# Six more output pieces kept as halves, and a wait ahead of GpSimd's second piece set

## The chip, the cores and the metric

The kernel runs on one core of a Trainium2 chip. The metric is the device time of one execution in microseconds, the median of three runs. Lower is better.

## What is computed

One layer of a mixer over 4096 frames of 1024 channels, then a last norm. Cut to what matters here:

```python
h = rms_norm(x, norm_w) * (1.0 + scale) + shift
gq, gk, gv, gz, glr, hq, hf, hi, hz, mg = split(h @ w_in)
# two gated linear recurrences over chunks of 64 frames; their decays:
log_a = log_sigmoid(glr @ gla_wa2 + gla_ba) / 16
log_f = logaddexp(log(lb), log1p(-lb) + log_sigmoid(hf))
g_a, g_b = split(sigmoid(mg + merge_b))
m = g_a * (o_g @ w_up_gla) + g_b * (o_h @ w_up_hgrn)
x = x + gate * (m @ w_out)          # 1024 x 1024, the "output" product
return rms_norm(x, final_norm_w)
```

## The kernel before

The 4096 frames are 8 blocks of 512. In each block TensorE walks through 75 slots. A slot is one weight tile of 128 partitions x 1024 numbers (512 KB) and the matmuls that use it. Slots 0 to 3 are hf, 4 and 5 gk, 6 to 9 hi, 10 to 13 gv, 14 and 15 gq, 16 to 19 hq, 20 to 27 the gates, 28 to 60 the merge gates and the up projections, and 61 to 74 (`OUT0` is 61) the output product. Slots 0 to 33, 59 and 60 hold 24 matmuls each (5.44 us); an output slot holds 12 (2.72 us). The 14 output slots are seven products of a Strassen-like scheme, two slots (q = 0, 1) for each: the first three multiply parts of m, the other four sums of them.

All matmuls are fp32r with each operand as a high and a low half, three products for each pair. So each weight tile needs two halves in SBUF, `w_hi` and `w_lo`, each a ring of 3 (`RING`). They come in one of two ways:

- From raw: SyncE (SP) loads the tile into `w_raw` (ring of 4, `RAW`), ScalarE copies it to `w_hi` (`split_hi`, L748) and VectorE subtracts to get `w_lo` (`split_lo`, L1024). Both do this right after the slot three places before has ended (`slot_done`). SP loads the tile that stands four raw uses ahead, when the split of the tile of this slot is done (`w_split`).
- From halves: in block 0 the split halves of the slots in `HALVES` are stored to DRAM (`keep_halves`, two stores of 512 KB at the slot, ahead of the raw load of that slot, L429). In later blocks `load_halves` (L444) brings them back, two loads of 512 KB, issued when the slot three places before has ended. Then ScalarE and VectorE do nothing for the tile. ScalarE's split of slot s in block 0 waits until the halves of slot s - 3 have been stored (`halves_kept`), since it overwrites them.

SP's queue is in order: what stands behind a wait is issued after it. In each block it also loads, around the output slots, the next block's transposed x (`xf`, two pairs at slots 55 and 58 and one at 63) and the residual `xy`, 512 KB for each of four frame tiles: two at slot 63 after `up_used`, two at slot 65 after `s_lo_done`. In `body` of SP the steps of one slot stand in this order: raw load, load of halves, xf, xy.

VectorE adds the finished output banks into `xy` (`bank_adds`, L1158). The first two adds stand at slot 64, behind the split for slot 67, and wait for the first two xy loads. TensorE's slot 67 waits for these two adds (`BANK_READ[3]` is 2), slot 69 for four, slot 71 for eight.

The weights of the output slots are not the input's: GpSimd makes them in block 0 (`out_pieces`), multiplied with the gate and combined, and stores 14 pieces to DRAM (`pieces`). It makes two sets, q = 0 and q = 1, each with four loads, eight elementwise operations on 128 x 1024 numbers and seven stores. The buffer `w_b` lies where ScalarE writes `o_tm` from slot 21 on.

The decays are worked out in slots 4 to 16, by ScalarE and VectorE in turn. TensorE's running sums of them are hosted behind slots 14, 15 (L1679, L1680) and 16 (L1687, L1688); those of slot 15 wait for VectorE's `pk` (L1302), which reads the bank. Near the end of that chain VectorE writes `la_lo` (L1286, slot 13), which is `la_split`.

## Time and profile before

| | us |
|---|---|
| median of 3 runs | 2816.75 (2815.58 to 2817.88) |
| profiled execution, its own time | 2816.22 |
| its span, first to last instruction | 2814.5 |
| TensorE busy in the span | 2771.9 |
| VectorE busy | 1708.7 |
| ScalarE busy | 1332.2 |
| GpSimd busy | 402.6 |

The profiled execution lies 0.5 us under the median and 1.7 us over its span. TensorE is busy 98% of the span, the DMA queue of SP takes 52.3% of the 16 DMA engines' time. Lines as L1583 are lines of the kernel before.

### The profile page before, as it was taken

The page shows a single profiled execution, that of the slowest core. Times are in us where ns is not written, and L with a number is a line of the kernel's source. Part 1 is how long each engine was busy: PE and PEld are TensorE (multiplying, and loading weights), DVE is VectorE, ACT ScalarE, POOL GpSimd, SP SyncE. Part 2 cuts the span into 40 slices and gives each one's busy share as a digit, 9 for nine tenths or more (in the row PEclk, how much of TensorE's full clock was granted, in tenths as well). Part 3 has the DMA queues.
Part 4 walks back from the last instruction along what each step waited for, and adds up shares of the span by engine and source line. Part 5 has one row for each costly group of instructions (what it writes and reads, how often), then busy time and mean ns, then how long its engine had stood idle before and what let it go on. Part 6 is the DMA issues. An engine that isn't in the chain of part 4 may idle for free.

```text
span 2814.5 us, 39321 instructions
## 1 busy us (share of the span) xinstructions
PE 2771.9 (98%) x15840; PEld 2339.1 (83%) x15840; DVE 1708.7 (61%) x2269; ACT 1332.2 (47%) x1854; POOL 402.6 (14%) x451
## 2 busy tenths in 40 slices
PE   6999999999999999999999999999999999999998
PEld 4778888889887898879888798888988889888897
DVE  7855484476744766547655577545675366744666
ACT  4643356344472454724547244463454534544344
POOL 1625310111001110011000110001101011000111
PEclk9999999999999999999999999999999999999999
DMA  9768574445734447344573456734566344653444
GB/s 375 284 237 300 203 246 181 151 156 166 256 135 165 152 169 271 124 163 155 191 277 108 148 160 213 244 125 142 163 214 234 128 149 152 227 187 136 149 154 176
DMA packets 154134, 532.34 MB, mean 189 GB/s; under 512 B 16288, under 2 KB 16544, under 8 KB 152416
## 3 DMA queue, kind: packets, MB, share of 16 engines
q1 hardware_dynamic: 147072, 505.50, 52.3%
q0 software_dynamic: 6624, 24.12, 2.4%
q8 instruction: 126, 2.06, 0.3%
q14 instruction: 56, 0.46, 0.0%
q10 hardware_dynamic: 256, 0.20, 0.0%
HBM read 473.85 MB, written 55.71 MB: 188 GB/s over the span
## 4 chain that ended last, share of the span: by engine, by line
PE 87%; ACT 5%; DVE 5%; issue 2%; DMA 1%; SPq 0%; POOL 0%; POOLq 0%; DVEq 0%; ACTq 0%
PE A L1458 28%; PE F L1469 16%; PE A L1561 10%; PE A L1583 7%; PE F L1500 6%; PE R L1500 5%; PE A L1500 3%; PE F L1458 3%; PE F L1583 2%; PE R L1613 1%; DVE w_lo L1024 1%; ACT w_hi L748 1%; PE F L1640 1%; PE A L1655 1%; PE F L1634 1%
## 5 line engine op out<-in xcount | busy, mean ns | idle before, releaser
L1024 DVE TENSOR_TENSOR w_lo<-w_raw,w_hi 128x1024 fp32r<-128x1024 f32 x423 | 550.2, 1301 | 397.1 <-ACT w_hi L748 395.8
L748 ACT ACTIVATE w_hi<-w_raw 128x1024 fp32r<-128x1024 f32 x423 | 446.9, 1057 | 494.9 <-PE R L1500 149.7
L1458 PE MATMUL A<-w_hi,h_hi 128*128 128x512 f32 (+1 forms) x1408 | 532.8, 378 | 0.0
L1458 PE MATMUL A<-w_lo,h_hi 128*128 128x512 f32 (+1 forms) x1408 | 523.1, 371 | 0.0
L1458 PE MATMUL A<-w_hi,h_lo 128*128 128x512 f32 (+1 forms) x1408 | 522.8, 371 | 0.0
L1458 PEld LDWEIGHTS A<-w_hi,h_hi 128*128 128x128 f32 x1408 | 264.4, 188 | 55.8 <-issue 8.7
L1458 PEld LDWEIGHTS A<-w_hi,h_lo 128*128 128x128 f32 x1408 | 264.4, 188 | 46.6
L1458 PEld LDWEIGHTS A<-w_lo,h_hi 128*128 128x128 f32 x1408 | 264.7, 188 | 42.8 <-issue 0.2
L1469 PE MATMUL F<-h_hi,w_hi 128*128 128x512 f32 x736 | 290.7, 395 | 0.0
L1469 PE MATMUL F<-h_lo,w_hi 128*128 128x512 f32 x736 | 287.3, 390 | 0.0
L1469 PE MATMUL F<-h_hi,w_lo 128*128 128x512 f32 x736 | 287.3, 390 | 0.0
L1561 PE MATMUL A<-o_hi,w_hi 128*128 128x512 f32 x512 | 199.4, 390 | 0.0
L1561 PE MATMUL A<-o_lo,w_hi 128*128 128x512 f32 x512 | 199.4, 390 | 0.0
L1561 PE MATMUL A<-o_hi,w_lo 128*128 128x512 f32 x512 | 199.2, 389 | 0.0
L1469 PEld LDWEIGHTS F<-h_hi,w_hi 128*128 128x128 f32 x736 | 138.7, 188 | 29.5 <-DVE w_lo L1024 0.4
L1469 PEld LDWEIGHTS F<-h_hi,w_lo 128*128 128x128 f32 x736 | 138.4, 188 | 29.3
L1469 PEld LDWEIGHTS F<-h_lo,w_hi 128*128 128x128 f32 x736 | 138.6, 188 | 28.1 <-issue 0.2
L601 POOL TENSOR_TENSOR rstd<-ssq,eps_t 128x4 f32<-128x4 f32 x64 | 33.9, 530 | 760.4 <-DVE ssq L1347 760.4
L1216 DVE TENSOR_TENSOR gates<-gates,A 128x512 f32<-128x512 f32 x128 | 82.2, 683 | 78.4 <-PE A L1561 78.4
L691 POOL TENSOR_TENSOR m_raw<-m_raw 128x256 f32<-128x256 f32 x24 | 24.2, 1007 | 704.4 <-DVE m_lo L1233 704.4
L1334 DVE SCALAR_TENSOR_TENSOR S_h<-S_h,a_cols,R 128x128 f32<-128x128 f32 x256 | 71.9, 343 | 78.8 <-PE R L1613 77.6
L881 ACT ACTIVATE gates<-F,col 128x512 f32<-128x512 f32 x44 | 30.3, 688 | 185.1 <-PE F L1469 185.1
(278 smaller groups left out, 5651.2 us busy)
## 6 DMA issues: line engine op xcount, KB each, us to landing
w_raw<-in_w_stream SPq DMA_DIRECT2D x225, 512.0 KB, 3.9
w_hi<-halves SPq DMA_DIRECT2D x154, 512.0 KB, 3.7
w_lo<-halves SPq DMA_DIRECT2D x154, 512.0 KB, 4.6
w_raw<-pieces SPq DMA_DIRECT2D x112, 512.0 KB, 5.3
w_raw<-m_pieces SPq DMA_DIRECT2D x84, 512.0 KB, 3.5
xy<-in_x SPq DMA_DIRECT2D x32, 512.0 KB, 6.5
result<-xy SPq DMA_DIRECT2D x32, 512.0 KB, 8.1
xf<-in_xt SPq DMA_DIRECT2D x30, 512.0 KB, 5.3
```

What stands on the lines that cost most here:

```text
L601: nc.gpsimd.tensor_tensor(dst, src, eps_t[:, 0:k], ALU.add).then_inc(pool_pow, 1)
L748: AF(w_hi[:, s % RING, 0:n], w_raw[:, r, 0:n], ACT.Copy).then_inc(w_hi_done, 1)
L881: AF(gates[:, j % 2, g, :], F[g][:, :], ACT.Sigmoid, bias=merge_b[:, g * KT + FEAT[j]:g * KT + FEAT[j] + 1]).then_inc(mg_used.sem, 1)
L1024: V.tensor_tensor(w_lo[:, s % RING, 0:n], w_raw[:, u % RAW, 0:n], w_hi[:, s % RING, 0:n].bitcast(fp32), ALU.subtract).then_inc(w_split, 1)
L1216: ins = V.tensor_tensor(gates[:, j % 2, g, :], gates[:, j % 2, g, :], A[2 * (j % 2) + g][:, :], ALU.mult)
L1334: ins = V.scalar_tensor_tensor(out=S_h[:, c, g, :], in0=S_h[:, 1 - c, g, :], scalar=a_cols[:, g, n:n + 1], in1=R[c][:, g * P:(g + 1) * P], ...
L1458: last = mm(banks[t][:, 0:width], src[ia][:, k, t * P:(t + 1) * P], w_[iw][:, s % RING, kk * width:(kk + 1) * width], start=(k == 0 and n ...
L1469: last = mm(dst[:, :], w_[iw][:, s % RING, k * P:(k + 1) * P], h_[ia][:, k, :], start=(k == 0 and n == 0), stop=(k == KT - 1 and n == 2))
L1500: last = mm(dst, w_[iw][:, s % RING, 512 * g + kk * P:512 * g + (kk + 1) * P], src[ia][:, kk // 2, kk % 2, :], start=(n < 4 and kk == 0 an ...
L1561: last = mm(A[2 * (j % 2) + g][:, :], w_[iw][:, s % RING, kk * P:(kk + 1) * P], o_[ia][:, kk, :], start=(k == 0 and n == 0), stop=(k == HE ...
L1583: last = mm(OUT_BANK[pair_][tt][:, :], src[ia][:, 2 * (2 * q + kk) + f, at:at + P], w_[iw][:, s % RING, kk * 512:(kk + 1) * 512], start=(f ...
L1613: last = mm(R[c][:, g * P:(g + 1) * P], kdec_h[fr, t, g * P:(g + 1) * P], v_h[fr, t, g * P:(g + 1) * P], start=True, stop=True)
```

## The change

`HALVES` grows by slots 61 to 66, `KEPT` and the DRAM tensor by the output slots; SP's one wait in block 1 now covers all stores. So in block 0 SP stores 12 more halves of 512 KB, at slots 61 to 66. In blocks 1 to 7 the six raw loads from `pieces`, the six copies on ScalarE and the six subtractions on VectorE go, and 12 loads of halves come. Separately, GpSimd waits for block 0's `la_split` before the first multiplication of its second set; the four loads of that set are issued before the wait.

```diff
-KEPT = range(RING, OUT0)
-HALVES = (*range(3, 10), *range(20, 36), 60)
+KEPT = range(RING, SLOTS)
+HALVES = (*range(3, 10), *range(20, 36), *range(60, 67))
...
-        halves = nc.dram_tensor("halves", [OUT0 - RING, 2, P, SLOT_W], fp32, kind="Internal").ap()
+        halves = nc.dram_tensor("halves", [SLOTS - RING, 2, P, SLOT_W], fp32, kind="Internal").ap()
...
-                                sp.wait_ge(halves_kept[r], 32 * stored_on(OUT0 + (r - OUT0) % RING))
+                                sp.wait_ge(halves_kept[r], 32 * stored_on(SLOTS + r))
...
+                    if q:
+                        pool.wait_ge(la_split.sem, la_split.at(0, 1))
                     for i, piece in ((0, B11), (2, B21), (3, B22)):
                         gated(i, q)
                         store(i, piece + q)
```

SP's queue in block 0 around the first output slots, before (the `xf` at the top stands at slot 60; `halves<-` is a store, `w_raw<-` a load):

```order
L455 DMA xf<-in_xt 128x1024
L423 DMA w_raw<-pieces 128x1024 x3
L455 DMA xf<-in_xt 128x1024
L555 DMA xy_106<-in_x 128x1024 x2
L423 DMA w_raw<-pieces 128x1024 x2
L555 DMA xy_107<-in_x 128x1024 x2
```

The same place now, up to the stores of slot 64:

```order
L455 DMA xf<-in_xt 128x1024
L429 DMA halves<-w_hi 128x1024
L429 DMA halves<-w_lo 128x1024
L423 DMA w_raw<-pieces 128x1024
L429 DMA halves<-w_hi 128x1024
L429 DMA halves<-w_lo 128x1024
L423 DMA w_raw<-pieces 128x1024
L429 DMA halves<-w_hi 128x1024
L429 DMA halves<-w_lo 128x1024
L423 DMA w_raw<-pieces 128x1024
L455 DMA xf<-in_xt 128x1024
L555 DMA xy_106<-in_x 128x1024 x2
```

Two stores of 512 KB now stand ahead of each raw load of slots 61 to 66.

SP's queue in a later block around the same slots, before (`w_hi<-halves` and `w_lo<-halves` are the load for slot 60; the second `xf` stands at slot 63):

```order
L444 DMA w_hi<-halves 128x1024
L444 DMA w_lo<-halves 128x1024
L423 DMA w_raw<-pieces 128x1024
L455 DMA xf<-in_xt 128x1024
L423 DMA w_raw<-pieces 128x1024 x4
L455 DMA xf<-in_xt 128x1024
L555 DMA xy_106<-in_x 128x1024 x2
L423 DMA w_raw<-pieces 128x1024 x2
L555 DMA xy_107<-in_x 128x1024 x2
```

Now, from the load for slot 63 on:

```order
L444 DMA w_hi<-halves 128x1024
L444 DMA w_lo<-halves 128x1024
L444 DMA w_hi<-halves 128x1024
L444 DMA w_lo<-halves 128x1024
L444 DMA w_hi<-halves 128x1024
L444 DMA w_lo<-halves 128x1024
L444 DMA w_hi<-halves 128x1024
L444 DMA w_lo<-halves 128x1024
L455 DMA xf<-in_xt 128x1024
L555 DMA xy_106<-in_x 128x1024 x2
L555 DMA xy_107<-in_x 128x1024 x2
L423 DMA w_raw<-pieces 128x1024 x4
```

The four pairs are the halves of slots 63 to 66, each behind a wait for the end of slots 60 to 63, and `xf` and `xy` now stand behind the last of these waits.

## Rows read from the trace of the kernel before

**Rows 1.** The page, part 1: busy us, share of the span, instructions.

```profile
PE 2771.9 (98%) x15840; PEld 2339.1 (83%) x15840; DVE 1708.7 (61%) x2269; ACT 1332.2 (47%) x1854; POOL 402.6 (14%) x451
```

**Rows 2.** Waits of TensorE over the whole span: us in total, times, longest.

```profile
PE R L1679 <- DVE pk L1302: 5.0, 1, 5.0
PE F L1583 <- DVE w_lo L1024: 2.7, 7, 0.4
```

**Rows 3.** The chain, slot 65 of blocks 2 and 3: start, us, what.

```profile
1060.15 5.73 PE F L1583 x24
...
1403.74 5.73 PE F L1583 x24
```

**Rows 4.** Stretches: slots 14-17 of blocks 0, 1; output slots of blocks 2, 7.

```profile
core 0: us, PE busy (x) PEld busy (x) DVE busy (x) ACT busy (x) POOL busy (x), PEclk, DMA share, GB/s
129.40:150.43 21.03, 16.02 (x65) 12.83 (x64) 15.49 (x10) 9.62 (x13) 19.04 (x13) 0.84 0.61 221
484.80:498.87 14.07, 14.07 (x64) 11.41 (x65) 8.65 (x10) 9.91 (x14) 0.00 (x0) 1.00 0.21 76
1048.29:1087.84 39.55, 39.04 (x169) 31.38 (x169) 36.72 (x44) 22.17 (x26) 0.10 (x1) 1.00 0.74 252
2764.79:2803.00 38.21, 38.19 (x168) 31.11 (x167) 30.25 (x36) 19.43 (x23) 0.74 (x2) 1.00 0.50 170
```

**Rows 5.** Timeline of VectorE, block 0 (126 to 142), then block 1.

```profile
126.83 3.42 DVE L1296 SCALAR_TENSOR_TENSOR y_g<-y_g,t 128x1024 f32<-128x1024 f32 x1
...
140.15 1.40 DVE L1302 SCALAR_TENSOR_TENSOR pk<-R,keep,pk 128x512 f32<-128x512 f32 x2
...
484.67 1.22 DVE L1296 SCALAR_TENSOR_TENSOR y_g<-y_g,t 128x1024 f32<-128x1024 f32 x1
```

**Rows 6.** Timeline of GpSimd, first and last of the second set's eight operations.

```profile
125.45 3.72 POOL L638 TENSOR_TENSOR w_b<-w_b,gate_bc 128x1024 f32<-128x1024 f32 x1 [1.51 <-DMA w_b<-in_w_stream]
...
149.98 2.42 POOL L659 TENSOR_TENSOR w_b<-w_b 128x1024 f32<-128x1024 f32 x1
```

**Rows 7.** Timeline of SP, slots 57 to 65 of block 2: start, us, issue.

```profile
1034.55 0.32 SPq L444 DMA_DIRECT2D w_hi<-halves  x1
1034.91 0.43 SPq L444 DMA_DIRECT2D w_lo<-halves  x1
...
1053.85 0.91 SPq L555 DMA_DIRECT2D xy<-in_x  x2
```

**Rows 8.** The page, part 6: DMA issues, KB each, median us to landing.

```profile
w_lo<-halves SPq DMA_DIRECT2D x154, 512.0 KB, 4.6
```

**Rows 9.** DMA issues from 853.5 to 854.4: one pair of halves.

```profile
w_lo<-halves SPq DMA_DIRECT2D x1, 512.0 KB, 6.3
```

**Rows 10.** Timeline of VectorE, block 2: the first adds into xy.

```profile
1064.55 1.28 DVE L1158 TENSOR_TENSOR xy<-xy,A 128x512 f32<-128x512 f32 x2
```

**Rows 11.** Timeline of TensorE: first matmuls of slots 61, 67 (block 2), 69 (block 0).

```profile
1048.29 0.47 PE L1583 MATMUL A<-w_hi,m_hi 128*128 128x512 f32 x1
...
1065.98 0.47 PE L1583 MATMUL A<-w_hi,s_hi 128*128 128x512 f32 x1
...
384.32 0.39 PE L1583 MATMUL A<-w_hi,s_hi 128*128 128x512 f32 x1
```

**Rows 12.** DMA issues from 355 to 356, block 0: the xf of slot 60.

```profile
xf<-in_xt SPq DMA_DIRECT2D x1, 512.0 KB, 6.4
```

**Rows 13.** Stretches of block 0 with a full DMA queue, columns as rows 4.

```profile
60.00:98.00 38.00, 38.00 (x213) 32.36 (x212) 26.34 (x27) 19.73 (x25) 11.08 (x9) 1.00 1.00 370
74.00:94.00 20.00, 20.00 (x104) 16.95 (x104) 9.84 (x8) 11.87 (x17) 7.17 (x7) 1.00 1.02 397
57.00:73.00 16.00, 16.00 (x94) 14.06 (x93) 13.84 (x19) 6.54 (x9) 0.21 (x1) 1.00 0.95 333
```

**Rows 14.** The page, part 5: groups, busy us, mean ns, idle before and what ended it.

```profile
L1024 DVE TENSOR_TENSOR w_lo<-w_raw,w_hi 128x1024 fp32r<-128x1024 f32 x423 | 550.2, 1301 | 397.1 <-ACT w_hi L748 395.8
L748 ACT ACTIVATE w_hi<-w_raw 128x1024 fp32r<-128x1024 f32 x423 | 446.9, 1057 | 494.9 <-PE R L1500 149.7
```

## The prediction

> **What bounds the kernel now.** I read the page's busy times first. TensorE is busy 2771.9 us of a span of 2814.5 [rows 1], so an edit can give back little: only the time in which it stands or runs at half clock. The chain shows slot 65 of blocks 2 and 3 at 1060.15 and 1403.74 [rows 3]: a steady block takes 343.59 us, and its end costs no more than what lies between its slots. Then I read the waits of TensorE [rows 2]. Past the start of the program, whose waits the change doesn't touch, two belong to it: one of 5.0 us in block 0, on VectorE's `pk`, and seven of 0.4 us on a weight split, at slot 65 of a block each. Last I read stretches. The part of slots 14 to 17 takes 21.03 us in block 0 and 14.07 in block 1 with the same matmuls; its clock is 0.84 against 1.00, so after it had stood TensorE ran for a while at 1.2 GHz in place of 2.4 [rows 4]. The 14 output slots take 39.55 us in block 2 and 38.21 in block 7, where no next block is prepared; 14 slots of 2.72 would be 38.1. So the first edit can give back at most some 1.45 us a block, the second at most 21.03 - 14.07 = 6.96 us, once.
>
> **The wait on GpSimd.** In block 0 VectorE's operations with two inputs in SBUF take 3.42 us beside GpSimd's second set, the same operation in block 1 takes 1.22; `pk`, with one input in a bank, keeps its 0.70 each [rows 5]. GpSimd's set starts at 125.45 and ends at 152.4 [rows 6]. Now it starts at `la_split`. Without it, `y_g` ends at 126.83 + 1.22 = 128.05, the next split at 129.3, and `la_lo` (after ScalarE's copy of about 1.1) near 130.6. That is where the set now starts. The split for slot 17 still falls beside it: it starts near 131.2, takes 3.4, and two `pk` of 1.40 end near 136.0. TensorE comes to them at 135.8 and waits 0.2 to 0.8 us in place of 5.0, and its clock stays up. Gain: **6.2 us**. If slot 16's `pk` is late in the same way and part of the half-clock stretch stays, it is 4; at best 7. The set ends 5.2 us later, with its last store near 161. ScalarE needs the buffer in slot 21, after 170, and SP needs the pieces at slot 57: neither waits.
>
> **The six splits that go, in blocks 1 to 6.** They free ScalarE and VectorE of six operations each a block, and with them the 0.4 us of slot 65. Their end has its price in SP's queue. The halves of slot s are loaded when slot s - 3 has ended. For slots 63 to 66 only two output slots of 2.72 us lie between, 5.44 us. SP issues 0.2 us after the end of a slot; `w_lo` is issued 0.36 after `w_hi` [rows 7] and lands 4.6 after that [rows 8]: 5.15 us. So the halves come in time by 0.3 us in the middle case. But a `w_lo` with nothing ahead of it but its other half can also take 6.3 [rows 9]; no row groups how often, and I take a quarter of the pairs to be late by 1 to 1.5 us.
>
> The larger price is the residual. In block 2 xy was issued at 1053.85 [rows 7]. It now stands behind the wait for the end of slot 63, behind the halves of slot 66 and one xf. Slot 61 starts at 1048.29 [rows 11], slot 63 ends 8.16 later at 1056.45, `w_hi` is issued at 1056.65, `w_lo` lands 4.95 later at 1061.6. Then come xf and two xy. One after another, 512 KB take 1.3 us at 397 GB/s [rows 13]: the second xy lands at 1065.5. VectorE's two adds take 1.28 [rows 10], two wake-ups 0.2, so slot 67, which waits for both, starts at 1067.0, where it started at 1065.98 [rows 11]: +1.0. VectorE was ready at 1060, it is the transfer that is last. Late halves push the end of slot 63 and the queue behind it; with four pairs, a quarter of them late by 1 to 1.5 us against 0.3 of slack, I add 0.6. So **+1.6 us a block**, 0.7 if no pair is late, 2.6 if two are. From slot 67 on nothing is late: VectorE has a split (1.22) and two adds (1.28) a slot of 2.72, and the raw tile of slot 71 lands near 1069. Six blocks: +9.6.
>
> The Trainium skill (DMA: Bandwidth & Descriptors, Anatomy of one DMA) puts a transfer at 2.0 us plus its bytes by 436 GB/s. For a pair of halves that would be 4.4 us; the rows show 4.95, so by the page the halves would have 0.8 us to spare in place of 0.3 and the term would be near +1.0 a block.
>
> **Block 7.** No xf stands ahead of xy, but the slots had no stall to give back either [rows 4]. By the same steps: slot 61 at 2764.6, slot 63 ends at 2772.8, `w_lo` at 2777.9, two xy at 2780.5, adds and wake-ups 2782.0, against 2781.0 before; with 0.6 for late pairs **+1.6**.
>
> **The stores in block 0.** This is the dearest part. Between the xf of slot 60, issued at 355.17 and landed 6.4 later at 361.6 [rows 12], and the last store of slot 66 stand 22 transfers of 512 KB: 12 new stores, five raw loads, one xf and four xy. All of them are issued by 376, since their splits are done by then, so the queue runs without a gap. At 397 GB/s, the row with the same mix of stores and loads, each takes 1.32 us and the last lands at 390.6; at 370 (1.42) 392.8, at 333 (1.57) 396.2 [rows 13]. ScalarE's split for slot 69 waits for that store: copy 1.06, VectorE's subtraction 1.3 [rows 14], then the two adds that stand behind it in VectorE's queue and that slot 69 waits for too, 1.28, and wake-ups: 394.4, against 384.32 before [rows 11]. **+10 us**, up to 15 by the slowest row; the low end is 6, if stores overlap loads better than any of these rows shows. On the way slot 67 waits for the store of slot 64; that is inside this sum. The queue has run down by slot 70 and nothing more is added. If TensorE's clock falls once more after standing, as it did in block 0, some 2 us come on top (6.96 less the 5.0 that it stood) [rows 2, 4].
>
> **Sum.** Against the profiled execution's 2816.2: -6.2 + 10 + 9.6 + 1.6 = +15.0, so 2831.2; the median stands 0.5 above the profiled one: 2831.8, say **2832**. With the ends: -7 + 6 + 4.2 + 0.7 = +4, and -4 + 16.5 + 15.6 + 2.6 = +31; all ends at once is unlikely, and I take 2823 to 2843 as this case's own range.
>
> **Rivals.** First, **faster**: the queue keeps up. It needs halves that land within 5.44 us nearly always, an xy that lands within some 7 us of its issue (it took 6.5 in the middle, with less ahead of it), and stores that don't hold up block 0. It decides at the start of slot 67: if both adds are done by then, that slot starts 16.3 us after slot 61 in place of 17.7. Then the gain is 7 + 7 x 1.45 = 17 us: 2800. For it speaks that VectorE, which is 36.7 of 39.55 us busy there [rows 4], is freed of a fifth; against it the order of SP's queue, which alone gives 1067.0. Chance 0.12.
>
> Second, **no change**: the same steps with the low ends, halves never late and xy 0.8 us earlier than I reckon (+0.2 a block), and block 0's stores costing 5 or 6, so that the decays' 6.2 pay for them: about 2817, from 2811 to 2822. Chance 0.14.
>
> Third, **a slower queue**. While both halves of every slot are read, 1.05 MB in 2.72 us is 385 GB/s, near the 397 that rows show and above 370 and 333 [rows 13]. At 352, the middle of the two slower rows, a pair takes 2.98 us: the fourth pair is 0.8 late and three more transfers 0.5, +1.3 a block more; block 0's 22 transfers take 1.49 each, 4 us more. Together 7 x 1.3 + 4 = +13: 2845. The Trainium skill (DMA: Bandwidth & Descriptors, Specifications) gives about 358 GB/s as the HBM limit of a core. The rows with 370 and 397 over 38 and 20 us speak against that as a ceiling for one core alone. Chance 0.10.
>
> **How the numbers follow.** Forecast 0.64, no change 0.14, faster 0.12, slower queue 0.10. A measurement here tells 0.2% (5.6 us) from no change: faster is below 2811, slower above 2822.4. So faster 0.12, same 0.14, slower 0.74. The range goes from 2811, which leaves out the faster case, to 2846, which leaves out the top of the slow ones.
>
> **What would show it.** In the changed profile: the wait of 5.0 us on `pk` gone or under 1 us, and slots 14 to 17 of block 0 in 14 to 16 us at full clock; the SP timeline with xy issued after slot 63's end; in blocks 1 to 6 TensorE waiting at slot 67 on VectorE's adds into xy, these in turn on the xy transfer, and a block of about 345.2 us; in block 0 ScalarE waiting on the stores `halves<-w_lo` ahead of the splits for slots 67 to 69, and block 1 starting some 4 us later. It is wrong if xy is still issued early, if stores and loads overlap to more than 420 GB/s, or if TensorE waits at slots 64 to 66 for halves by more than a microsecond each.

## The result, and the profile after

The changed kernel takes **2849.55 us** (median of 5 runs, 2846.36 to 2857.59) against 2817.06 for the kernel before in the same measurement: ratio 1.0117, 95% interval 1.0102 to 1.0132. It is slower, as forecast, but by 32.5 us where the forecast said 15, and it lies above the range of 2811 to 2846. The profiled execution took 2849.55 us as well, with a span of 2847.8 and a mean granted clock of 0.991. Behind the edit of GpSimd's code all line numbers are two higher, so the output slots' matmul is L1585 and the add into `xy` L1160.

The busy times are the answer to [rows 1]. TensorE has the same 15840 matmuls and 8.5 us more of busy time: some of them ran at half clock.

```profile
PE 2780.4 (98%) x15840; PEld 2345.5 (82%) x15840; DVE 1656.6 (58%) x2227; ACT 1292.8 (45%) x1812; POOL 400.0 (14%) x451
```

TensorE's waits over the whole span, the answer to [rows 2] (us in total, times, longest): the 5.0 us on `pk` are gone, and the splits of slot 65 wait once in place of seven times. In their place stand 27.2 us for the adds into `xy`, nine times, and 4.7 us for late halves.

```profile
PE A L1585 <- DVE xy L1160: 27.2, 9, 7.1
...
PE A L1585 <- DMA w_lo<-halves: 3.0, 6, 0.8
PE F L1585 <- DMA w_lo<-halves: 1.7, 2, 1.4
...
PE F L1585 <- DVE w_lo L1026: 0.4, 1, 0.4
```

Stretches of the changed kernel, the answer to [rows 4] with the same columns: slots 14 to 17 of block 0, then the 14 output slots of blocks 0, 2, 3 and 7.

```profile
130.08:143.79 13.71, 13.71 (x66) 11.38 (x65) 9.55 (x8) 8.49 (x12) 11.47 (x7) 1.00 0.73 270
354.48:406.85 52.37, 42.01 (x169) 33.25 (x169) 36.80 (x44) 22.16 (x26) 0.11 (x1) 0.90 0.84 321
1056.55:1100.29 43.74, 40.44 (x170) 32.44 (x168) 30.91 (x38) 17.79 (x21) 0.11 (x1) 0.96 0.78 269
1404.19:1446.09 41.90, 38.96 (x170) 31.30 (x168) 30.90 (x38) 17.80 (x21) 0.11 (x1) 1.00 0.80 283
2795.22:2835.38 40.16, 38.78 (x169) 31.19 (x167) 25.89 (x32) 15.51 (x19) 0.75 (x2) 1.00 0.57 210
```

The first row is the gain: 13.71 us, at clock 1.00, without a wait, where it was 21.03. Of these 7.3 us some 6.7 are left at slot 61, since TensorE came to the stretch 0.7 us later: that much its start of the program, which the change doesn't touch, was longer in this execution. The others are the losses. The output slots of a block I call its tail, from the first matmul of slot 61 to the first matmul of the next stage (of block 7: to its end). Before, a tail is 39.45 us in block 0, 39.55 in blocks 1 to 6 and 38.35 in block 7. Block 3 (41.90) and block 2 (43.74) differ mainly in the clock, which is 0.96 in block 2: of the 1.84 us between them 1.6 lie behind the start of slot 67.

The whole difference of the two spans is 33.3 us, by the starts of stages in both traces:

| place | us |
|---|---|
| start to slot 61 of block 0 | -6.7 |
| tail of block 0 (52.37 against 39.45) | +12.9 |
| tails of blocks 1 to 6 (41.9, 43.7, 41.9, 43.7, 45.1, 46.2) | +25.2 |
| tail of block 7 | +1.8 |
| between the tails, 0.13 us shorter in blocks 1 to 6 | -0.8 |
| behind TensorE's last matmul | +0.9 |

**What makes a tail longer in a steady block.** The chain of waits in block 2, the answer to [rows 3] (start, us, what):

```profile
1056.71 8.17 PE A L1585 x36
...
1066.69 8.67 DMA xy<-in_x
...
1075.98 0.69 DVE xy L1160
1076.67 0.14 issue
1076.81 3.45 PE A L1585 x10
```

The chain goes from the end of slot 63 (36 matmuls) over SyncE's queue into the second transfer of xy, which takes 8.67 us from issue to landing; then come the add and slot 67, at 1076.81, 20.26 us after slot 61's start at 1056.55. Before it was 17.69 us (1065.98 - 1048.29 in [rows 11]).

SyncE's queue in block 3, the answer to [rows 7] (start, us, issue). The halves of slot 66 are issued when slot 63 has ended, 8.36 us after slot 61's start at 1404.19; xf and four xy follow with no gap. In block 2 of the kernel before the first xy was issued 5.6 us after slot 61's start.

```profile
1412.55 0.32 SPq L444 DMA_DIRECT2D w_hi<-halves  x1
1412.91 0.44 SPq L444 DMA_DIRECT2D w_lo<-halves  x1
1413.39 0.43 SPq L455 DMA_DIRECT2D xf<-in_xt  x1
1413.87 1.91 SPq L555 DMA_DIRECT2D xy<-in_x  x4
```

DMA issues in four short stretches around these, for `w_lo`, xf, the first and the second xy (the last number is us from issue to landing):

```profile
w_lo<-halves SPq DMA_DIRECT2D x1, 512.0 KB, 5.2
...
xf<-in_xt SPq DMA_DIRECT2D x1, 512.0 KB, 6.8
...
xy<-in_x SPq DMA_DIRECT2D x1, 512.0 KB, 7.5
...
xy<-in_x SPq DMA_DIRECT2D x1, 512.0 KB, 8.4
```

Counted from slot 61's start they land at 13.95, 16.0, 17.15 and 18.56 us. Before, the second xy of block 2 landed at 12.9, while VectorE was still busy with splits: its adds began at 16.3 [rows 10], so TensorE didn't wait for a transfer there.

**What makes it longer in block 0.** ScalarE's timeline (the brackets give the idle time and its releaser): it stands 8.90, 2.63 and 5.17 us behind the stores of `w_lo` halves, ahead of the splits of slots 67, 68 and 69.

```profile
375.32 1.06 ACT L750 ACTIVATE w_hi<-w_raw 128x1024 fp32r<-128x1024 f32 x1 [8.90 <-DMA halves<-w_lo]
379.00 1.06 ACT L750 ACTIVATE w_hi<-w_raw 128x1024 fp32r<-128x1024 f32 x1 [2.63 <-DMA halves<-w_lo]
385.24 2.25 ACT L750 ACTIVATE w_hi<-w_raw 128x1024 fp32r<-128x1024 f32 x2 [5.17 <-DMA halves<-w_lo]
```

TensorE's timeline at the starts of slots 67 and 69, the answer to the last row of [rows 11]:

```profile
379.05 0.76 PE L1585 MATMUL A<-w_hi,s_hi 128*128 128x512 f32 x1 [7.05 <-DVE xy L1160]
...
388.97 0.77 PE L1585 MATMUL A<-w_hi,s_hi 128*128 128x512 f32 x1 [2.89 <-DVE xy L1160]
```

Both first matmuls take 0.76 us and more, where that of [rows 11] takes 0.47: TensorE is at half clock. Four stretches of the changed kernel with the granted clock at 0.50, in block 0 (two), 2 and 6; blocks 4 and 5 have one of 3.4 us like block 2, blocks 1 and 3 have none:

```profile
375.00:381.80 6.80, 2.75 (x7) 2.21 (x8) 3.65 (x4) 2.12 (x2) 0.00 (x0) 0.50 1.03 420
388.70:392.10 3.40, 3.13 (x8) 2.50 (x9) 3.40 (x5) 0.04 (x1) 0.00 (x0) 0.50 0.72 261
1078.20:1081.60 3.40, 3.40 (x9) 2.62 (x9) 1.93 (x3) 0.45 (x1) 0.00 (x0) 0.50 0.72 207
2467.40:2474.20 6.80, 6.12 (x15) 4.79 (x16) 4.00 (x5) 0.62 (x1) 0.00 (x0) 0.50 0.67 258
```

TensorE had stood 2.7 us for slot 67 of block 2, and 1.4 us after it went on the clock was at 1.2 GHz for 3.4 us: the slots from 67 to 69 took 1.6 us more than before. In block 3 it had stood 2.76 us in the same place and the clock stayed at 2.4 GHz. The Trainium skill (TensorE: Matmul & The Clock Gate, Part 1) says that an idle TensorE goes to the lower clock, and that the number of matmuls which run at that clock at a kernel's start differs from run to run. Here it is two blocks of one execution that differ, after nearly the same standing.

### The profile page after: what moved, and what is told of

It is laid out like the page before. It is cut to its first block, busy times and chain, and to the rows that moved or that the text cites. A ratio compares the mean times of both kernels' runs of the same rounds, so it can differ in the third digit from the quotient of the medians.

```text
span 2847.8 us, 39285 instructions
## 1 busy us (share of the span) xinstructions
PE 2780.4 (98%) x15840; PEld 2345.5 (82%) x15840; DVE 1656.6 (58%) x2227; ACT 1292.8 (45%) x1812; POOL 400.0 (14%) x451
## 4 chain that ended last, share of the span: by engine, by line
PE 89%; ACT 4%; DMA 3%; DVE 2%; issue 1%; SPq 1%; POOL 0%; POOLq 0%; DVEq 0%; ACTq 0%
PE A L1460 28%; PE F L1471 17%; PE A L1563 12%; PE A L1585 8%; PE F L1502 6%; PE R L1502 5%; PE A L1502 3%; PE F L1460 3%; DMA xy<-in_x 2%; PE R L1615 1%; PE F L1642 1%; PE A L1657 1%; PE F L1636 1%; DMA ada_w<-in_ada 1%; ACT w_hi L750 1%
## 5 line engine op out<-in xcount | busy, mean ns | idle before, releaser
L1026 DVE TENSOR_TENSOR w_lo<-w_raw,w_hi 128x1024 fp32r<-128x1024 f32 x381 | 496.6, 1305 | 434.5 <-ACT w_hi L750 434.2
L750 ACT ACTIVATE w_hi<-w_raw 128x1024 fp32r<-128x1024 f32 x381 | 403.3, 1059 | 543.7 <-PE A L1585 143.4
L1585 PE MATMUL A<-w_hi,s_hi 128*128 128x512 f32 x256 | 105.1, 410 | 27.2 <-DVE xy L1160 27.2
```

Source lines behind the costliest of these rows:

```text
L750: AF(w_hi[:, s % RING, 0:n], w_raw[:, r, 0:n], ACT.Copy).then_inc(w_hi_done, 1)
L1026: V.tensor_tensor(w_lo[:, s % RING, 0:n], w_raw[:, u % RAW, 0:n], w_hi[:, s % RING, 0:n].bitcast(fp32), ALU.subtract).then_inc(w_split, 1)
L1585: last = mm(OUT_BANK[pair_][tt][:, :], src[ia][:, 2 * (2 * q + kk) + f, at:at + P], w_[iw][:, s % RING, kk * 512:(kk + 1) * 512], start=(f ...
```

## The experiments

Times are medians; the kernel before, measured beside them, took 2815.8 to 2819.4. "One run" is one execution; five executions of the changed kernel spread over 11 us (2846.4 to 2857.6), so a single run within that spread can't be told from it by its time. Where a block is named, "lands at" counts from the start of its slot 61.

**1. The new wait alone.** The kernel before with nothing but GpSimd's wait for `la_split`.

```diff
+                    if q:
+                        pool.wait_ge(la_split.sem, la_split.at(0, 1))
```

> The kernel before with GpSimd's wait alone; no more halves. The changed kernel reached slot 61 of block 0 at 354.5 us in place of 361.2, so this edit should be worth 6.7 us, once: 2810.3. If the gain in the changed kernel had another cause (the halves free nothing before slot 58 of block 0, so I see none), it would be 0. Slots 14 to 17 of block 0: 14 us in place of 21; every later block 343.6 us.

Measured: 2809.29 us (10 runs), ratio 0.9974, interval 0.9964 to 0.9983; slot 61 of block 0 starts at 354.92 in place of 361.19. The wait is worth 6.3 us in the trace and 7.8 between the medians, and no part of the loss is its own.

**2. The halves alone,** without the new wait.

```diff
-                    if q:
-                        pool.wait_ge(la_split.sem, la_split.at(0, 1))
```

> The changed kernel without GpSimd's wait. If the two edits don't touch each other: 2849.5 + 6.7 = 2856, with the wait of 5.0 us on pk back in block 0 and the ends of all blocks as in the changed kernel (slot 67 of blocks 1 to 6 starting 20 to 21.5 us after slot 61). Rival: GpSimd's later stores of pieces are part of the crowd in block 0; then its end gets shorter here than the 52.4 us of the changed kernel.

Measured: 2856.38 us, one run; the wait of 5.0 us on `pk` is back. The tails are 50.0 in block 0, 45.8, 47.5, 41.9, 43.3, 41.7 and 43.8 in blocks 1 to 6, and 41.3 in block 7. The two edits add up: the halves cost 40.3 us with the wait (2849.55 - 2809.29) and 39.3 without it.

**3. The stores without the loads.** Block 0 stores the halves of slots 61 to 66; the later blocks load and split these slots raw, as before.

```diff
-    return s not in HALVES
+    return s not in HALVES or s >= OUT0
...
-    return s in KEPT and not from_raw(1, s)
+    return s in KEPT and s in HALVES
```

> The changed kernel with the 12 stores of slots 61 to 66 in block 0 (never read again) and those slots from raw in all blocks. It parts the price of the stores from that of the loads. If the stores alone hold up block 0: its last 14 slots take 52.4 us as in the changed kernel, blocks 1 to 7 are those of before, total 2817 - 6.7 + 12.9 = 2823. If the loads in later blocks had no part in it the total would be 2849; if the stores had none, 2810.

Measured: 2821.6 us, one run. Its output slots, block 0 and block 3 (columns as [rows 4]):

```profile
354.38:405.92 51.54, 41.69 (x170) 33.00 (x170) 36.63 (x44) 22.19 (x26) 0.11 (x1) 0.90 0.88 325
1397.21:1436.78 39.57, 39.12 (x169) 31.39 (x169) 36.89 (x44) 22.14 (x26) 0.11 (x1) 1.00 0.75 253
```

The stores lengthen block 0 by 12.1 us and nothing else. Against run 1 that is the whole 12.3 us between the medians. So the loss has two separate parts, and some 28 us of it (2849.55 - 2821.6) belong to the loads in blocks 1 to 7.

**4. xf issued behind the first two xy,** which moves one transfer out of xy's way.

```diff
-                    if s in (63, 74) and not last:
-                        ...  load_pair(b + 1, n + 1)
                     if s in (63, 65):
                         ...
+                    if s in (63, 74) and not last:
+                        ...  load_pair(b + 1, n + 1)
```

> The changed kernel with the load of xf at slot 63 put behind the first two loads of xy in SP's queue; nothing else. Theory of the queue (slot 67 starts when the second xy has landed, plus 1.4 us of adds): the second xy lands one transfer earlier, 17.3 us after slot 61 starts, slot 67 starts 1.3 us earlier in blocks 1 to 6, and where the standing gets shorter TensorE's clock falls in fewer blocks: 2849.5 - 8 - 0 to 6, so 2836 to 2842. Rival (late halves of slots 63 to 66 set the start of slot 67): unchanged, 2849.

Measured: 2830.59 us, one run: 19 us of the 32 come back. The second xy lands at 16.7 to 18.6, TensorE's waits for the adds fall to 14.6 us from 27.2, the tails of blocks 1 to 6 are 40.0 to 41.9, and no block after block 0 has a stretch at half clock. Block 0, where xf moves too, takes 50.1.

One transfer less ahead of xy is worth about 1.3 us a block in its landing and, with the clock that then holds, more than that in time. The transfer that was taken out of the way is the slow one, as this run shows too: from 16 to 18 us after slot 61's start, where xf now stands, the queue moves 305 to 351 GB/s in blocks 1 to 6, against 388 to 420 in the changed kernel (block 3; the last number is GB/s):

```profile
1414.31:1416.31 2.00, 2.00 (x11) 1.65 (x10) 0.01 (x1) 0.97 (x1) 0.00 (x0) 1.00 0.98 315
```

**5. xy late, nothing else.** Run 1 with both first xy held until slot 63 has ended; no output slot is loaded as halves.

```diff
                         if s == 63:
                             sp.wait_ge(up_used.sem, up_used.at(b, 8))
+                            if b:
+                                sp.wait_ge(slot_done, DONE[b, 63])
```

> The kernel before with GpSimd's wait, and in blocks 1 to 7 SP waits for the end of slot 63 ahead of the first two xy loads, as in the changed kernel; no further halves. It parts the late issue of xy from what stands ahead of it. Theory of the queue: with no pair of halves ahead, the second xy lands near 15.5 us after the start of slot 61 in place of 12.9, adds 1.4 later, just before slot 67 would start (17.7): at most 0.5 us a block, 2809 to 2813. Rival, the late issue alone is the price: slot 67 at 20 us and more, 2.3 or more a block, 2824 and up.

Measured: 2809.33 us, as run 1 to 0.04. The xy are issued at 8.5 and 8.9 and land at 12.1 and 13.4 in block 3, and the tails of blocks 1 to 6 stay at 39.5 to 39.6. The second xy of block 3, from issue to landing:

```profile
xy<-in_x SPq DMA_DIRECT2D x1, 512.0 KB, 4.5
```

So the later issue by itself costs nothing. VectorE's adds come in time with a landing at 13.4; it takes the later landing, 18.6 in place of 13.4 with nearly the same issue, to make TensorE wait.

**6. Only slots 61 and 62 as halves.**

```diff
-HALVES = (*range(3, 10), *range(20, 36), *range(60, 67))
+HALVES = (*range(3, 10), *range(20, 36), *range(60, 63))
```

> The changed kernel with only slots 61 and 62 added to the halves. Their loads are issued at the ends of slots 58 and 59, with 24-matmul slots between, and nothing stands behind a later wait: xy issued as before (5.6 us after slot 61 starts). Theory: no load of halves is late; slot 61 starts 0.15 us earlier, VectorE has two splits less, so the 0.7 us before slot 65 shrinks: 0.2 to 0.8 us less a block; block 0 has four stores more with time for them. 2803 to 2808. Rival (any further halves hold up the queue): above 2812.

Measured: 2799.68 us, one run. Block 0, then block 3:

```profile
353.40:392.89 39.49, 38.97 (x169) 31.31 (x169) 36.72 (x44) 22.07 (x26) 0.11 (x1) 1.00 0.87 321
1381.05:1419.26 38.21, 38.21 (x169) 31.45 (x168) 35.25 (x42) 21.69 (x25) 0.11 (x1) 1.00 0.74 252
```

Here the edit does its whole good: TensorE is busy in all of the 38.21 us, each slot takes 2.72, and the four stores in block 0 delay nothing. The queue is ahead again before xy is due: the first two are issued at 4.2 and 4.7 and land at 10.2 and 11.5.

**7. The first two xy ahead of the wait for slot 63** and of the halves of slot 66.

```diff
+                    if b and s == 63:
+                        sp.wait_ge(up_used.sem, up_used.at(b, 8))
+                        for t in (0, 1):
+                            sp.dma_start(xy(t), x[bass.ds(b * T + t * P, P), :]).then_inc(xy_in[0].sem, 16)
                     if not first and s + RING in KEPT and not from_raw(b, s + RING):
...
-                    if s in (63, 65):
+                    if s == 65 or s == 63 and not b:
```

> The changed kernel with the first two xy loads of blocks 1 to 7 ahead of the wait for slot 63 and of the halves for slot 66. If the order alone were the trouble, both adds are done 15 us after slot 61 starts and slot 67 starts at 17 or earlier: 2820. If it is the amount in the queue, the standing moves: the halves of slot 66 land behind xy at 15.7 in place of 13.5, slot 66 waits for them by about 2 us, slot 67 starts near 19: 2826 to 2834, with TensorE's waits on a DMA of halves and no longer on the adds.

Measured: 2840.89 us, one run. xy now lands at 12.8 and 14.1 in block 3 and slot 67 of blocks 1 to 7 waits no more, but slot 66 waits for its own halves. TensorE's waits:

```profile
PE F L1589 <- DMA w_lo<-halves: 15.9, 10, 2.4
```

In the chain of block 3 the `w_lo` of slot 66 takes 7.97 us from its issue, with two xy ahead of it. The order in the queue chooses who waits. The tails of blocks 1 to 7 are 41.2 to 43.2.

**8. Only slot 65 as halves, xf behind xy** as in run 4.

```diff
-HALVES = (*range(3, 10), *range(20, 36), *range(60, 67))
+HALVES = (*range(3, 10), *range(20, 36), 60, 65)
```

> The changed kernel with only slot 65 added to the halves, and xf of slot 63 behind xy. Slot 65 is the one that waits 0.4 us for VectorE in the kernel before. Its halves are loaded at the end of slot 62, one pair alone; xy is issued 0.3 us later than before. Theory: the pair lands 10.6 us after slot 61 starts and slot 65 needs it at 11.3, the second xy lands at 13.2 or so, VectorE's chain is one split shorter: slot 67 starts 0.5 to 1 us earlier, 2804 to 2807. Rival (halves with two short slots between are late as such): slot 65 waits 0.5 us or more, 2810 and up.

Measured: 2809.11 us, one run, no better than run 1. The slot that had waited (65) waits no more, and slot 71 starts 0.6 to 0.9 us late in its place: it waits for adds that stand behind a split whose raw tile comes late. The tails of blocks 1 to 6 are 39.2 to 39.9, that of block 0 is 40.2. With xf moved as well this is two edits in one run; it shows that relieving the slot that waits gained nothing here, where relieving the first two did (run 6).

**9. Half the bytes.** The halves of slots 63 to 66 are loaded for 512 of their 1024 columns; the rest of the tile keeps what stood there, and the sums are not the reference's.

```diff
-                n = slot_width(s)
+                n = 512 if 63 <= s <= 66 else slot_width(s)
```

> The changed kernel with the loads of the halves of slots 63 to 66 in blocks 1 to 7 cut to the first 512 of 1024 columns, so half the bytes; the other half of each tile is what the slot three before left there, all matmuls run as before. Theory (bytes in the queue): each pair lands 1.3 us sooner, no slot waits for halves, xf and xy follow at once, the second xy lands near 16.2 us after slot 61 starts and slot 67 starts at 17.6, about where it started in the kernel before: the last 14 slots of blocks 1 to 6 take 39.2 to 39.8, total 2820 to 2826 (block 0 keeps its 6 us). Rival (the number of issues or the wait order, not the bytes): 41.9 to 46 a block, 2843 to 2850.

Measured: 2847.51 us, one run, within 2 us of the changed kernel. Block 3, a half of slot 66 (`w_lo`) and the second xy, from issue to landing:

```profile
w_lo<-halves SPq DMA_DIRECT2D x1, 256.0 KB, 2.8
...
xy<-in_x SPq DMA_DIRECT2D x1, 512.0 KB, 8.6
```

The halves land in time and no slot up to 66 takes more than 2.72 us. Yet the second xy lands at 17.8 to 18.8, nearly as late as the 18.6 to 18.8 of the changed kernel's blocks 1 to 4. That the sum of bytes ahead of xy makes it late was my reading until then; it fell.

**10 and 11. Three and four slots as halves:** the table of run 6 with `range(60, 64)` and `range(60, 65)`.

> Slots 61, 62 and 63 added to the halves. Slot 63 is the first with only two output slots between issue and use: 5.4 us against 5.2 for a pair in the middle case. Theory: block 0 gets two stores more with little room, slot 63 waits now and then by up to 1 us, the rest has no excess: 2800 to 2804, slower than two slots. Rival (VectorE's relief pays for more): below 2799.5.

> Slots 61 to 64 added to the halves: two pairs with short lead, and xy issued behind the end of slot 61, so hardly later. Theory: 0.3 to 1 us of waits for halves a block, xy one or two transfers later but still in time; block 0's stores of slots 63 and 64 begin to hold up the split of slot 67: 2802 to 2812. If the price came only with the full queue of slots 65 and 66 it would be 2800; if it grows evenly from two to six slots (50 us over four), 2825.

Measured, one run each: 2806.19 and 2814.18 us. With three, block 0 already takes 41.3 and block 1 39.9, the others 38.3 to 38.6. With four, block 0 takes 47.5 and blocks 1 to 6 38.7 to 40.2. The stores of block 0 (0, 1.9, 8.0, 12.9 us for two, three, four and six slots) cost more the more there are. The loads begin to cost at three, where slot 63 was late by 1.7 us in block 1 and 0.4 in block 6, and cost 0.5 to 2.0 us in each of blocks 1 to 6 with four.

**12. Slots 61 and 62 once more,** the code of run 6.

> The kernel with slots 61 and 62 alone and GpSimd's wait once more, timed against the kernel before. One look gave 2799.7 with every output slot of blocks 1 to 7 at 2.72 us. It should hold: 2798 to 2802, 0.6% faster than before.

Measured: 2800.49 us (2800.19 to 2801.73, 5 runs), ratio 0.9944, interval 0.9930 to 0.9958. It beats both kernels.

**13 and 14. The third and fourth xy held back** until slot 65 has ended, with all and with half of the halves' bytes.

```diff
                             if s == 65:
+                                if b and t == 2:
+                                    sp.wait_ge(slot_done, DONE[b, 65])
                                 sp.wait_ge(s_lo_done.sem, s_lo_done.at(b, t - 1))
```

> The changed kernel, but in blocks 1 to 7 the third and fourth load of xy (issued 10.6 and 11.1 us after the start of slot 61) wait until slot 65 is through, so that only xf and the first two xy stand in the queue together. Theory BUNCH (transfers that stand together share the engines, so the second xy is slowed by the two behind it): the second xy lands about 1.5 us sooner, 17 us in place of 18.6 to 19.8 after the start of slot 61, the gap before slot 67 falls from 5.7 to about 4, and the tail of a steady block from 43.8 us to about 42. Rival ORDER (each transfer is served in the order of issue, those behind cost nothing): the second xy lands at 18.6 or later as before, the tails stay within 0.5 us of the changed kernel's, and the time is 2845 to 2852.

> As the run before, and the halves of slots 63 to 66 are loaded for 512 of their 1024 columns (the rest is left out, so the output is not the reference's). BUNCH: with half the bytes ahead and the last two xy out of the way the second xy lands 4 to 5 us after its issue, near 15 us after the start of slot 61, and slot 67 waits under 1 us more than its share. ORDER: as with half the bytes alone, landing at 18.3 to 18.8.

Measured: 2847.91 us (4 runs, 2846.2 to 2851.15) and 2846.1 (one run). The second xy lands at 18.4 to 20.9 and 17.9 to 19.1 in blocks 1 to 6. Holding back what stands behind the second xy didn't make it land sooner: BUNCH fell, ORDER holds.

**15. All five together, no halves.** Run 1, with xf and the four xy issued one behind the other once slot 63 has ended and `s_lo` is done.

```diff
+                    if s == 63 and b:
+                        sp.wait_ge(slot_done, DONE[b, 63])
+                        sp.wait_ge(s_lo_done.sem, s_lo_done.at(b, 1))
+                        sp.wait_ge(s_lo_done.sem, s_lo_done.at(b, 2))
...
-                        for t in (0, 1) if s == 63 else (2, 3):
+                        for t in ((0, 1, 2, 3) if s == 63 else ()) if b else (0, 1) if s == 63 else (2, 3):
```

> The kernel before with the later start of the decays; no output slot is loaded as halves. In blocks 1 to 7 xf and all four xy are issued one right behind the other at the end of slot 63 (some 8.5 us after the start of slot 61). BUNCH (five transfers of 512 KB that stand together suffice to make the second xy late, whatever is ahead): the second xy lands 8 us or more after its issue, at 17 or later, the gap before slot 67 is 4 us or more, tails about 41.5. Rival HALVES (it takes the halves in the queue ahead): the second xy lands within 6 us of its issue, under 15.5, and the tails stay at 39.6.

Measured: 2839.72 us, one run. `s_lo` was later than I had thought, so that xf was issued at 10.8 and the second xy at 11.7. In block 3 xf, first and second xy, with nothing ahead of them, take from issue to landing:

```profile
xf<-in_xt SPq DMA_DIRECT2D x1, 512.0 KB, 4.5
...
xy<-in_x SPq DMA_DIRECT2D x1, 512.0 KB, 5.4
...
xy<-in_x SPq DMA_DIRECT2D x1, 512.0 KB, 6.2
```

The second xy takes 6.2 us, short of the 8 that BUNCH asked and longer than the 6 that HALVES allowed, and it lands at 17.8 since it was issued late; neither is borne out by it. The order of the queue is: 4.5 us for xf out of an idle queue (4.3 to 4.7 in blocks 1 to 6), then one transfer each 1.28 us. In block 7 no xf stands ahead and the first xy leaves an idle queue too; it takes less:

```profile
xy<-in_x SPq DMA_DIRECT2D x1, 512.0 KB, 3.5
```

The kernel before had shown this price of xf already. Its load at slot 55 finds the queue idle and takes 4.3 to 4.5 us in each of blocks 1 to 6 (the first row, block 3), where the 84 loads from `m_pieces` take 3.5 in the middle (the second, from the page):

```profile
xf<-in_xt SPq DMA_DIRECT2D x1, 512.0 KB, 4.4
...
w_raw<-m_pieces SPq DMA_DIRECT2D x84, 512.0 KB, 3.5
```

(Its tails, 43.3 to 45.0, say nothing of halves: the raw loads stand behind all five, and TensorE waits for them at slot 68.)

**16. Another source.** The xf issued in slot 63 and the xy of blocks 1 to 7 read kept halves in place of the inputs, so that the sums are not the reference's.

```diff
+                if nb > 1 and j == 2:
+                    src = halves[0, 0, :, 0:1024]
...
+                            src = halves[1 + t, 0, :, 0:1024] if b else x[bass.ds(b * T + t * P, P), :]
```

> The changed kernel, but in blocks 1 to 7 the xf load issued in slot 63 and the four xy loads read kept halves in place of the inputs (the same 512 KB each into the same tiles; the output is not the reference's). In the changed kernel the packets of the stretch from 12 to 15 us after the start of slot 61 take 175 to 273 ns and move 213 to 324 GB/s, where those before and behind take 142 to 150 ns at over 400. Theory SOURCE (the first packets that read the inputs x and x transposed are slow, wherever they stand): with the halves as source there is no such stretch, the second xy lands 0.9 to 1.3 us sooner, near 17.4 us after the start of slot 61, and the gap before slot 67 falls from 5.7 to about 4.6. Rival PLACE (the dip belongs to that moment, to the tiles written or to what the engines do then): it is there as before and the second xy lands at 18.6 and later.

Measured: 2839.42 us, one run. In the changed kernel the stretch from 12 to 15 us after the start of slot 61 of block 3 and the four us after it (the last three numbers are granted clock, share of the DMA engines and GB/s):

```profile
1416.19:1419.19 3.00, 3.00 (x15) 2.47 (x14) 1.23 (x1) 1.06 (x2) 0.00 (x0) 1.00 0.96 285
1419.19:1423.19 4.00, 2.25 (x10) 1.52 (x9) 0.41 (x1) 1.69 (x2) 0.00 (x0) 1.00 1.01 413
```

The first of these stretches with the other source (the four us after it run at 413 GB/s here too):

```profile
1414.72:1417.72 3.00, 3.00 (x15) 2.45 (x15) 1.22 (x1) 1.38 (x2) 0.00 (x0) 1.00 1.03 406
```

The DMA engines are busy in both, but with the inputs as source they move 285 GB/s in these 3 us and 406 without. That is 121 x 3 = 0.36 MB, which at 413 GB/s is 0.9 us. From issue to landing `w_lo`, xf and both xy take, in block 3:

```profile
w_lo<-halves SPq DMA_DIRECT2D x1, 512.0 KB, 5.1
...
xf<-halves SPq DMA_DIRECT2D x1, 512.0 KB, 5.9
...
xy<-halves SPq DMA_DIRECT2D x1, 512.0 KB, 6.7
...
xy<-halves SPq DMA_DIRECT2D x1, 512.0 KB, 7.5
```

They land at 13.78, 15.07, 16.34 and 17.63: one each 1.28 us behind `w_lo`, where in the changed kernel xf lands 2.05 us behind it. Block 3 shows the difference at its largest. In the mean of blocks 1 to 6 the rate from 12 to 15 us is 318 GB/s in the changed kernel and 379 with the other source, xf lands 1.9 and 1.6 us behind `w_lo`, and the second xy 4.5 and 4.1 behind it. In the blocks whose slots up to 65 aren't much late themselves it lands at 18.6 to 18.8 (changed, blocks 1 to 4) and 17.6 to 18.2 (blocks 2 to 5). SOURCE holds for that part. Block 1 took 43.9 us all the same, since its slot 63 started 2.1 us late for want of halves.

**17. The same rows touched before.** Three loads of 8 columns of the same rows, in SP's steps of slot 60.

```diff
+                    if s == 60 and b:
+                        sp.dma_start(warm[:, 0, :], xt[bass.ds((b + (not last)) * P, P), 4 * T:4 * T + 8]).then_inc(warmed, 16)
+                        sp.dma_start(warm[:, 1, :], x[bass.ds(b * T, P), 0:8]).then_inc(warmed, 16)
+                        sp.dma_start(warm[:, 2, :], x[bass.ds(b * T + P, P), 0:8]).then_inc(warmed, 16)
+                    if s == 62 and b:
+                        sp.wait_ge(warmed, 48 * b)
```

> The changed kernel, and in blocks 1 to 7 three loads of 8 columns each (32 bytes of each of 128 rows) of the same rows of x transposed and of x are issued in slot 60, some 3 us before the start of slot 61. Theory FIRST TOUCH (rows of an input are slow when first read): the dip goes and the second xy lands at about 17.5. Rivals: SOURCE without a memory of the touch, or PLACE: the dip stays, and the second xy lands at 18.6 or, by the cost of three more issues on SyncE's queue, up to 1 us later.

Measured: 2847.48 us, one run. The slow stretch, 12 to 15 us after slot 61's start in block 3, is still there:

```profile
1416.79:1419.79 3.00, 3.00 (x15) 2.46 (x14) 1.23 (x1) 1.33 (x2) 0.00 (x0) 1.00 0.94 288
```

The second xy lands at 18.6 in blocks 3 and 4 and later in the others. The three touches were issued 1.0 to 2.0 us behind slot 61's start in block 3, not ahead of it as expected, and landed by 5.9, over 3 us ahead of xf's issue at 9.3. Such a touch of 32 bytes a row did not help.

**18. Only xf from the other source;** the four xy read x.

```diff
+                if nb > 1 and j == 2:
+                    src = halves[0, 0, :, 0:1024]
```

> The changed kernel, but only xf (the load issued in slot 63 for the next block) reads kept halves in place of the transposed input, so that the next block's sums are not the reference's; the four xy read x as in the changed kernel. Where run 16 changed both sources, this one tells them apart. In blocks 1 to 4 of the changed kernel xf lands 1.5 to 2.5 us (mean 1.9) behind the last half and the second xy at 18.67 in the mean; where x came first (run 4) the first xy landed 1.25 us behind the last half in the mean and the second 1.4 to 1.9 behind that. XF (the slow packets are those of the transposed input): as in run 16, the stretch from 12 to 15 us moves about 400 GB/s, xf lands about 1.4 behind the last half and the second xy at about 17.9. XY or SWITCH (any first read of an input, whichever it is, is slow): the slow packets move to the first xy, and the second xy lands at 18.6 as before.

Measured: 2846.54 us, one run. The stretch from 12 to 15 us in block 5, where the slots before were not late:

```profile
2111.54:2114.54 3.00, 3.00 (x15) 2.26 (x14) 1.23 (x1) 1.39 (x2) 0.00 (x0) 1.00 1.01 408
```

In the mean of blocks 1 to 6 the rate is 366 GB/s (285 in block 6, though), xf lands 1.6 us behind `w_lo` and the second xy 4.2: nearly what run 16 gave with both sources changed. In the two blocks without late slots ahead (4 and 5) it lands at 17.8 and 17.9, with tails of 41.1 and 41.2. So XF holds: the slow load is that of the transposed input. The dip moves with xf in run 4, and out of an idle queue it takes 0.9 us more than others, in run 15 and in the kernel before. The time hardly moves nevertheless, since in this execution slots 62 to 64 of blocks 1, 2, 3 and 6 started late for want of halves and three of these blocks fell to half clock. The landing of xf is worth some 0.8 us of a block; late halves and the clock, which differ from one execution to the next, are worth more.

## Why the prediction was wrong, step by step

**The wait on GpSimd: right.** Forecast -6.2, measured -6.7 in the trace of the changed kernel and -6.3 in run 1. The stretch itself gained 7.3, more than the 7 that were the best case: 5.2 where the wait had ended, and 2.1 of half clock behind it. VectorE's timeline of block 0, the answer to [rows 5]: `y_g` takes 1.22, the split for slot 17 and `pk` fall beside GpSimd's set, and TensorE waits for neither, since `pk` is through at 136.0.

```profile
127.55 1.22 DVE L1298 SCALAR_TENSOR_TENSOR y_g<-y_g,t 128x1024 f32<-128x1024 f32 x1
...
131.92 2.76 DVE L1026 TENSOR_TENSOR w_lo<-w_raw,w_hi 128x1024 fp32r<-128x1024 f32 x1 [0.81 <-ACT w_hi L750]
134.60 1.40 DVE L1304 SCALAR_TENSOR_TENSOR pk<-R,keep,pk 128x512 f32<-128x512 f32 x2
```

**The stores of block 0: right in mechanism, 2.9 us short.** Counted from slot 61's start, the forecast put the last store's landing at 29.4 us and slot 69 at 33.2; they were at 30.7 and 34.5. That is 1.3 of the 2.9: the 22 transfers took 1.36 us each in place of 1.32. The other 1.6 are the clock, at half from 388.70 on in slot 69, which the prediction named as possible and left out of its sum. The half clock in slot 67 cost nothing, since slot 69 waited all the same. The order was as told: ScalarE behind the stores, VectorE's adds behind the split, TensorE behind the adds.

**Blocks 1 to 6: the step that failed.** Forecast +1.6 a block, 9.6 in all; measured +25.2. The path was right: slot 67 waits for the adds, these for the second xy, and xy for its place in SP's queue. What failed are the durations of the transfers ahead of it, and the clock after the standing, which the sum put at nothing. It splits in two at the start of slot 67.

Up to slot 67 the six blocks lose 17.5 us: 2.3 to 2.6 in blocks 1 to 4, 4.0 and 3.8 in blocks 5 and 6. The step "w_lo lands 4.95 later ... then come xf and two xy, one after another, 1.3 us each" gave 17.2 for the second xy; block 3 shows 18.56. Term by term: `w_lo` 5.6 us after its pair's first issue in place of 4.95 (+0.64), xf 2.05 behind it in place of 1.3 (+0.75), the two xy 2.56 in place of 2.6. The +0.75 is shown by runs 16 and 18 to come from the source of xf: with kept halves in place of the transposed input the second xy lands some 0.7 us sooner in undisturbed blocks. The sum had given xf the 1.3 us of any transfer of its size, though the trace before had it 0.9 slower than others out of an idle queue (run 15). The +0.64 is the halves themselves: the four pairs of block 3 take 4.7, 5.5, 5.8 and 5.6 us from the first issue to the last landing. I had taken 4.95 for all four, from the median of pairs that mostly stand 5.44 us apart; here one comes each 2.72 us, so that the next is issued before the last has landed. That this is why they are slower is argued, not shown. Between them they add 1.4 us a block at the landing, against which my 0.6 for late halves stood, of another cause. The estimate that the prediction took from the Trainium skill (DMA: Bandwidth & Descriptors, Anatomy of one DMA), 4.4 us for a pair, is fitted there to transfers that GpSimd issues; these are SyncE's, and no pair of block 3 was that fast. My 0.6 was right in kind in blocks 5 and 6 alone, where slot 65 or slot 63 started late: 1.4 us more in each than in the other four. In block 3 slots 64 and 65 were late by 0.3 each, all of it hidden by the wait for xy.

Behind slot 67 the six blocks lose another 7.7 us: 1.6 each in blocks 2, 4 and 5 and 2.9 in block 6. TensorE stood 2.4 to 3.0 us ahead of slot 67 in every block, and in four of six the clock fell to 1.2 GHz for 3.4 or 6.8 us. The prediction spoke of the clock in block 0 only. This was an error of reasoning, since my own sum already meant that TensorE would stand there: it put slot 67 at 18.7 us behind slot 61, with six slots of 2.72 between, which leaves 2.4 us of standing. I did not ask what that does to the clock. It was worth nearly as much as the term that I had worked out in detail.

**Block 7: right, in part by luck.** +1.6 forecast, +1.8 measured. No xf stands in the way, and the clock held through its slots. But the 0.6 for late pairs stood in for something else: no late start of slot 64 reached slot 67, while the last `w_lo` landed 0.6 us and the second xy 0.8 us later than the sum had them.

**The rivals.** Faster (2800): its condition, slot 67 at 16.3 us after slot 61, was not met by six slots of halves, and is met by two: run 6 and 12 gave 2799.7 and 2800.5, which was that rival's time. A slower queue (2845): its time was near, and so was its size, +1.3 a block at the landing of xy, but its mechanism was not. That rival had 352 GB/s throughout; in block 3 the queue moves 384 GB/s from 4 to 12 us after slot 61's start, while the pairs pass, 285 in the 3 us after that, where xf stands, and 413 to 420 behind it, above all of [rows 13]. Halving the bytes of the halves changed the landing by less than 1 us (run 9).

**What stays open.** Why the load of the transposed input is slow where it stands in the queue: whether by its layout, its place in memory, or otherwise, was not tried. Nor is it settled what made run 9 as slow as the changed kernel: its halves were in time, but xf landed 4.7 us behind `w_lo` in block 3 and 7.0 behind its own issue, with the queue at 228 GB/s from 11 to 14 us after slot 61's start, where the changed kernel moved 311. And in which block the halves of slots 62 to 64 come late and the clock falls, no run explains; it differs between executions that are otherwise alike.

## What to carry to other kernels

Replacing a load by two that must wait for a buffer turns a queue that ran ahead into one that follows the consumer; everything behind it in that queue, wanted or not, is then late, and what is late first is what the consumer needs next. Relieve as few slots as remove the wait: two of six gave the whole gain here (2800.5), since the queue recovered its lead before xy was due. Don't give all transfers of one size the same price: read it for each source from a place where the queue was idle, as 4.4 and 3.5 us could be read here before the change. And when a forecast makes TensorE stand for 2 to 3 us in each block, as here, it must carry the clock's price, here 1.6 us for 3.4 us at half clock, in some blocks and not in others.

## What the runs showed of the hardware

- The load of the transposed input was slower than others of its size (512 KB). Out of an idle queue it took 4.3 to 4.5 us (six times in the kernel before) and 4.3 to 4.7 (run 15), where loads from `m_pieces` took 3.5 in the middle and one of x 3.5 (run 15, block 7). With halves ahead of it the queue moved 285 to 354 GB/s from 12 to 15 us in blocks 1 to 6, the DMA engines 96% busy in block 3, where kept halves read into the same tile gave 356 to 406 (run 16); then 413. Moved back in the queue, it took the dip along (305 to 351 from 16 to 18 us, run 4).
- Loads of 512 KB that stood in one queue landed 1.28 us apart (runs 15 and 16), and holding back what stood behind them gained nothing (run 13). They landed mostly, not always, in order of issue: in block 5 of the changed kernel xf landed 0.13 us behind the first xy, which was issued after it, and in block 3 of run 9 the two landed within 0.04 us.
- Standing of about 2.7 us was followed by a fall to 1.2 GHz in block 2 and not in block 3 of the changed kernel; the clock fell after standing of 1.8 us in block 6 of run 7 and held after 3.1 in block 1 of run 18. In the changed kernel a fall lasted 3.4 or 6.8 us, and 3.4 us of it cost 1.6 where nothing else was waited for.
